# A two-layer retention and sliding-window kernel: splits, loads and statistics in another order

## The reference, cut

```python
def post_norm(res, out, g, b):
    z = DN_ALPHA * res + out
    mu = z.mean(-1, keepdims=True)
    var = jnp.square(z - mu).mean(-1, keepdims=True)
    return (z - mu) * lax.rsqrt(var + LN_EPS) * g + b

def retention_layer(x, w_in, w_out, pos):
    h = x @ w_in                                   # 1024 x 6144
    q, k, v, g = jnp.split(h, [1024, 2048, 4096], axis=-1)
    q = rope(q, pos); k = rope(k, pos) * RET_QK_DIM ** -0.5
    att = einsum('bhncd,bhnmd->bhncm', qc, kc) * dec      # per chunk
    inner = einsum('bhncm,bhnme->bhnce', att, vc)
    def step(state, (qn, kn, vn)):
        cross = einsum('bhcd,bhde->bhce', qn, state) * xi
        state = state * g_chunk + einsum('bhcd,bhce->bhde', kn * zeta, vn)
        return state, cross
    r = inner + cross; r = (r - mean(r)) * rsqrt(var(r) + GN_EPS)   # per head
    return (silu(g) * r) @ w_out                   # 2048 x 1024

def swa_layer(x, w_in, w_out, sinks, k_band, v_band, bias, key_valid):
    q, gate = jnp.split(x @ w_in, 2, axis=-1)      # 1024 x 2048
    sc = where(key_valid, q * SWA_HEAD_DIM ** -0.5 @ k_band + bias, NEG_INF)
    m = maximum(sc.max(-1), sink); p = exp(sc - m)
    o = (p / (p.sum(-1) + exp(sink - m))) @ v_band
    return (o * silu(gate)) @ w_out                # 1024 x 1024
```

## Time and profile before

| | us |
|---|---|
| median of three runs | 2483.75 |
| lowest, highest | 2483.28, 2490.3 |
| profiled execution, device time | 2483.47 |
| profiled execution, span | 2481.5 |

### The profile page before, as it was taken

The page is one execution under the profiler, slowest core; times in us unless marked ns, Lnnn a source line. Parts: engine busy times, 40 slices in busy tenths (PEclk is TensorE's granted clock), DMA queues, the critical chain, the costliest instruction groups (busy, mean ns, idle before and its releaser), DMA issues.

```text
span 2481.5 us, 30993 instructions
## 1 busy us (share of the span) xinstructions
PE 2341.3 (94%) x11506; PEld 1900.2 (77%) x11506; DVE 1812.3 (73%) x2578; ACT 1180.6 (48%) x1754; POOL 345.5 (14%) x352
## 2 busy tenths in 40 slices
PE   7889989989999999999999999999999999999995
PEld 5677777867778887787778888778777888878774
DVE  6977888755886668874697767886478667787457
ACT  3433345346544445534744544443664445553473
POOL 4212201113001110001201001100110110010122
PEclk9999999999999999999999999999999999999998
DMA  9786677571764445744274544575146444464413
GB/s 331 280 294 246 226 240 254 170 280 52 241 199 148 135 129 173 263 148 136 91 268 134 170 158 131 168 256 185 62 153 237 131 141 154 128 203 134 131 60 110
DMA packets 215061, 443.38 MB, mean 179 GB/s; under 512 B 15040, under 2 KB 52432, under 8 KB 211328
## 3 DMA queue, kind: packets, MB, share of 16 engines
q1 hardware_dynamic: 200832, 375.58, 46.1%
q0 software_dynamic: 14080, 65.83, 7.2%
HBM read 379.75 MB, written 57.41 MB: 176 GB/s over the span
## 4 chain that ended last, share of the span: by engine, by line
PE 58%; DVE 15%; issue 12%; DMA 7%; ACT 4%; POOL 2%; SPq 1%; POOLq 0%; DVEq 0%; ACTq 0%
PE accs L644 16%; PE accs L645 15%; PE accs L646 15%; DVE w_lo L1250 5%; DMA stage<-t_prep 4%; PE bank L644 2%; PE bank L646 2%; PE bank L645 2%; ACT w_hi L948 2%; PE bank L866 1%; DMA x_sums<-part_lo 1%; PE bank L875 1%; PE bank L885 1%; PE bank L730 1%; POOL rstd L1830 1%
## 5 line engine op out<-in xcount | busy, mean ns | idle before, releaser
L1250 DVE TENSOR_TENSOR w_lo<-stage,w_hi 128x1024 fp32r<-128x1024 f32 x536 | 670.4, 1255 | 414.3 <-ACT w_hi L948 413.2
L948 ACT ACTIVATE w_hi<-stage 128x1024 fp32r<-128x1024 f32 x536 | 563.6, 1057 | 585.3 <-DMA stage<-t_prep 273.3
L644 PE MATMUL accs<-w_hi,xs 128*128 128x512 f32 x1120 | 450.5, 402 | 45.2 <-DVE krT L1328 12.0
L646 PE MATMUL accs<-w_hi,xs 128*128 128x512 f32 x1120 | 442.6, 395 | 0.0
L645 PE MATMUL accs<-w_lo,xs 128*128 128x512 f32 x1120 | 442.4, 395 | 0.0
L644 PEld LDWEIGHTS accs<-w_hi,xs 128*128 128x128 f32 x1120 | 214.1, 191 | 100.1 <-issue 51.5
L644 PE MATMUL accs<-x_hi,w_hi 128*128 128x512 f32 (+1 forms) x640 | 248.8, 389 | 17.4 <-DVE qT L1714 16.3
L1830 POOL TENSOR_TENSOR rstd<-ve,half 128x1 f32<-128x1 f32 x96 | 80.7, 841 | 1265.1 <-DVE ve L1306 1215.5
L646 PEld LDWEIGHTS accs<-w_hi,xs 128*128 128x128 f32 x1120 | 213.7, 191 | 46.3
L645 PEld LDWEIGHTS accs<-w_lo,xs 128*128 128x128 f32 x1120 | 214.1, 191 | 42.5
L645 PE MATMUL accs<-x_lo,w_hi 128*128 128x512 f32 (+1 forms) x640 | 239.9, 375 | 0.0
(11 more groups left out here) (184 smaller groups left out, 3863.9 us busy)
## 6 DMA issues: line engine op xcount, KB each, us to landing
stage<-t_prep SPq DMA_DIRECT2D x224, 512.0 KB, 4.4
stage<-ret_w_in SPq DMA_DIRECT2D x96, 512.0 KB, 3.9
stage<-ret_w_in SPq DMA_DIRECT2D x128, 256.0 KB, 2.9
stage<-swa_w_in SPq DMA_DIRECT2D x64, 512.0 KB, 3.8
t_prep<-t_buf POOLq DMA_DIRECT2D x28, 1024.0 KB, 6.3
stage<-ret_w_out SPq DMA_DIRECT2D x48, 512.0 KB, 3.7
cs<-rope_t SPq DMA_DIRECT2D x16, 1024.0 KB, 7.6
t_buf<-ret_w_in POOLq DMA_DIRECT2D x32, 512.0 KB, 9.6
```

The lines of the kernel that those rows point to most:

```text
L644: mm(dst, lhs[0], rhs[0], start=start, stop=False, skip_group_check=reopened)
L646: return mm(dst, lhs[1], rhs[0], start=False, stop=stop, skip_group_check=reopened)
L948: copy(w_hi[:, g % HS], stage[:, g % LS], ACT.Copy).then_inc(w_hi_made, 1)
L1250: nc.vector.tensor_tensor(w_lo[:, g % LS], stage[:, g % LS], w_hi[:, g % HS].bitcast(F32), sub).then_inc(w_split, 1)
```

## The change

1. `RO_SPLITS`: split 3 of `ret_w_out`'s operand moves from RO + 5 to RO + 4; ACT's `norm_r(H - 1, 3)` moves from RO + 3 to RO + 4, behind two `copy_r`.
2. Next sums 2 and 3 move from Q0 + 2 and Q0 + 3 to Q1 and Q1 + 1, behind the softmax steps there; their stores move with them.
3. The eight loads of sums at a strip's first pair become two each at pairs 0, 2, 5 and 8.
4. The four part loads wait for the products of RO + 14, 17, 20 and 23.
5. The second layer's norm: the statistics of tile t + 1 stand between gain and bias of tile t (`ln_step`).
6. At RO + 24 the pair's `make_lo` stands between the bias of tile 0 and the gain of tile 1.
7. At SO: split 4 one pair later, the second `o_summed` sum at SO + 2 instead of SO + 1, at SO + 2 the output sum ahead of `make_lo`, at SO + 3 the sum ahead of the split; the half statistics of P2 move from SO + 5 to SO + 9.
8. In the seventh v/gate pair the scores stand ahead of `make_lo`.

The diff, cut (comments and declarations left out; `next_sum_lo` on DVE moves as `next_sum_hi` does on ACT):

```diff
-RO_SPLITS = {61: 0, 63: 1, 65: 2, 77: 3, 78: 4, 80: 5, ...
+RO_SPLITS = {61: 0, 63: 1, 65: 2, 76: 3, 78: 4, 80: 5, ...
-SO_SPLITS = {SO - 2: (0,), SO - 1: (1, 2), SO + 1: (3,), SO + 2: (4,), SO + 4: (5,), SO + 5: (6,), SO + 7: (7,)}
+SO_SPLITS = {SO - 2: (0,), SO - 1: (1, 2), SO + 1: (3,), SO + 3: (4,), SO + 4: (5,), SO + 5: (6,), SO + 7: (7,)}
+NEXT_SUMS = (Q0, Q0 + 1, Q1, Q1 + 1)
+SUM_LOADS = {0: 0, 2: 1, 5: 2, 8: 3}
...
-                    if s > 0 and p == 0:
-                        sp.wait_ge(products, used(s * NP - 1))
-                        wait_sums_stored(sp, s)
-                        for n in range(4):
-                            for hl in range(2):
-                                sp.dma_start(xs[:, X_SUM_SLOT[n], hl].bitcast(F32), x_sums_dram[n, hl])\
-                                    .then_inc(sums_loaded[n], 16)
-                    if s + 1 < NS and Q0 + 1 <= p <= Q0 + 4:
-                        n = p - Q0 - 1
+                    if s > 0 and p in SUM_LOADS:
+                        n = SUM_LOADS[p]
+                        if p == 0:
+                            sp.wait_ge(products, used(s * NP - 1))
+                            wait_sums_stored(sp, s)
+                        for hl in range(2):
+                            sp.dma_start(xs[:, X_SUM_SLOT[n], hl].bitcast(F32), x_sums_dram[n, hl])\
+                                .then_inc(sums_loaded[n], 16)
+                    if s + 1 < NS and p - 1 in NEXT_SUMS:
+                        n = NEXT_SUMS.index(p - 1)
...
-                    if p == RO + 3:
-                        norm_r(H - 1, 3)
                     if p == RO + 4:
                         copy_r(H - 1, 0)
                         copy_r(H - 1, 1)
+                        norm_r(H - 1, 3)
...
-                    if s + 1 < NS and Q0 <= p < Q0 + 4:
-                        next_sum_hi(s, p - Q0)
+                    if s + 1 < NS and p in NEXT_SUMS[:2]:
+                        next_sum_hi(s, NEXT_SUMS.index(p))
...
+                    if s + 1 < NS and p in NEXT_SUMS[2:]:
+                        next_sum_hi(s, NEXT_SUMS.index(p))
...
-                if i == 2 * n + 1:
+                if i == (2 * n + 1 if kind == "ro" else 4 * n + 1):
                     for t in range(2):
                         half_stats(s, kind, "P2", t, 0)
...
+            def ln_step(s, t):
+                dve.wait_ge(gb_loaded, 32 * (2 * s + 2))
+                if t == 0:
+                    ln_begin(s, 1, 0)
                 ln_gain(t)
+                if t + 1 < NT:
+                    ln_begin(s, 1, t + 1)
+                ln_bias(s, 1, t)
+            def ln_two_tiles(s, w, t, g=None):
                 ln_begin(s, w, t)
                 ln_gain(t)
                 ln_begin(s, w, t + 1)
                 ln_bias(s, w, t)
+                if g is not None:
+                    make_lo(g)
                 ln_gain(t + 1)
                 ln_bias(s, w, t + 1)
...
+                    score_first = h < RH and j == VG + 6
+                    if score_first:
+                        evacuate_score(H, 0)
+                        make_lo(g + AHEAD)
...
-                        if v == 6:
-                            evacuate_score(H, 0)
...
-                        ln_two_tiles(s, 0, 0)
-                        make_lo(g + AHEAD)
+                        ln_two_tiles(s, 0, 0, g + AHEAD)
...
                     if SO <= p < SO + 9:
                         output_sums(s, "so", p)
-                    for n in SO_SPLITS.get(p, ()):
-                        split_so(s, n)
-                    if p in (SO, SO + 1, SO + 3):
+                    if p == SO + 2:
+                        make_lo(g + AHEAD)
+                    if p != SO + 3:
+                        for n in SO_SPLITS.get(p, ()):
+                            split_so(s, n)
+                    if p in (SO, SO + 2, SO + 3):
...
+                    if p == SO + 3:
+                        split_so(s, SO_SPLITS[p][0])
...
                 wait_sums_stored(pool, s - 1)
+                pool.wait_ge(products, used((s - 1) * NP + RO + 14 + 3 * n))
```

More of the change, by code:

```diff
@@ L178 @@
             ("P7", 0), ("P7", 1), ("P3", 0), ("P3", 1), ("P4", 0), ("P4", 1)]
-RO_SPLITS = {61: 0, 63: 1, 65: 2, 77: 3, 78: 4, 80: 5, 81: 6, 82: 7, 85: 8, 86: 9, 87: 10, 89: 11, 90: 12, 92: 13}
+RO_SPLITS = {61: 0, 63: 1, 65: 2, 76: 3, 78: 4, 80: 5, 81: 6, 82: 7, 85: 8, 86: 9, 87: 10, 89: 11, 90: 12, 92: 13}
 RO_SUMS = {67: "S3A", 70: "S3B", 71: "S2A", 73: "S4A", 74: "S1A", 79: "S2B", 81: "S1B", 83: "S4B"}
 S3A, S3B, S2A, S4A, S1A, S2B, S1B, S4B = range(1, 9)
-SO_SPLITS = {SO - 2: (0,), SO - 1: (1, 2), SO + 1: (3,), SO + 2: (4,), SO + 4: (5,), SO + 5: (6,), SO + 7: (7,)}
+SO_SPLITS = {SO - 2: (0,), SO - 1: (1, 2), SO + 1: (3,), SO + 3: (4,), SO + 4: (5,), SO + 5: (6,), SO + 7: (7,)}
 TURN_BANK = (4, 6, 7, 4)
+NEXT_SUMS = (Q0, Q0 + 1, Q1, Q1 + 1)
+SUM_LOADS = {0: 0, 2: 1, 5: 2, 8: 3}
 def need(eng, sem, n):
@@ L1528, in ln_bias @@
                                                in1=gb[:, 1, :], op0=ALU.mult, op1=add).then_inc(ln_dve, 1)
-            def ln_tile(s, w, t):
-                dve.wait_ge(gb_loaded, 32 * (2 * s + w + 1))
-                ln_begin(s, w, t)
+            def ln_step(s, t):
+                dve.wait_ge(gb_loaded, 32 * (2 * s + 2))
+                if t == 0:
+                    ln_begin(s, 1, 0)
                 ln_gain(t)
-                ln_bias(s, w, t)
-            def ln_two_tiles(s, w, t):
+                if t + 1 < NT:
+                    ln_begin(s, 1, t + 1)
+                ln_bias(s, 1, t)
+            def ln_two_tiles(s, w, t, g=None):
                 dve.wait_ge(gb_loaded, 32 * (2 * s + w + 1))
@@ L1613, in _ @@
                         rope_k_products(H)
-                    if first_step(p) is None and p not in (RO + 24, KV - 1, KV + 2, KV + 3):
+                    score_first = h < RH and j == VG + 6
+                    if score_first:
+                        evacuate_score(H, 0)
+                        make_lo(g + AHEAD)
+                    if first_step(p) is None and p not in (RO + 24, KV - 1, KV + 2, KV + 3, SO + 2) and not score_first:
                         make_lo(g + AHEAD)
@@ L1619, in _ @@
                     if p < NT and s > 0:
-                        ln_tile(s - 1, 1, p)
+                        ln_step(s - 1, p)
                     if h < RH and j < VG:
@@ L1707, in _ @@
                         make_lo(g + AHEAD + 1)
-                    if s + 1 < NS and Q0 <= p < Q0 + 4:
-                        next_sum_lo(s, p - Q0)
+                    if s + 1 < NS and p in NEXT_SUMS[:2]:
+                        next_sum_lo(s, NEXT_SUMS.index(p))
                     if p in (Q0 + 3, Q1 + 3):
@@ L1747, in _ @@
                             out_, x, y, op = s2v, o_part(1, 4, 8), s3v, sub
-                        elif p == SO + 1:
+                        elif p == SO + 2:
                             dve.wait_ge(o_summed, 4 * s + 2)
```

## The result

| | median us | lowest, highest | runs |
|---|---|---|---|
| before | 2483.5 | 2477.4, 2490.4 | 6 |
| changed | 2464.2 | 2462.7, 2467.0 | 6 |

The ratio of changed to before is 0.9924, with a 95% interval of 0.9909 to 0.9938: 19 us faster, where 47 us were forecast. It lies 1.2 us outside the stated range (2419 to 2463). The profiled execution of the changed kernel took 2462.66 us, with a span of 2460.7 us (before 2481.5), so that the two traces differ by 20.8 us.

What follows compares the result with a forecast made beforehand. TensorE (PE), busy 94% of the span, was taken as the bound, so only its idle time and lower clock could be won. Seven terms summed to 47.2 us off 2483.47, giving 2436 us, range 2419 to 2463.

Steps and rivals of the forecast that it cites:

- Next sums behind the softmax: At Q1, PE's waits for qT shorten as sums 2 and 3 no longer delay ACT and DVE: 12.6 us, clock included.
- Heads of strips: First head, strips 1 to 3: PE's krT waits go, 7.0 us, plus 2.2 of clock in strip 3; together 9.2 us.
- the third rival: Slower: spread x sum loads and part loads meet weights where none met before, 3.78 us each; 2491 us, chance 0.05.
- Scores ahead of a weight split: At the score steps, nine att_lo waits shrink because DVE's weight split no longer stands ahead: 8.1 us.
- Split 3 a pair earlier: Seventh pair of ret_w_out: PE's wait for ra goes in three strips, 0.3 us left in strip 3; 8.5 us.
- Part loads: Stretch of four pairs: loads issued one per three pairs no longer delay weights; 5.5 us, clock included.
- Layer norm at RO + 24: At the 25th pair the w_lo wait goes, but the k/v pair still waits behind bias loads: 1.5 us of 6.7.
- SO: Second layer's output (swa_w_out): z wait of 1.18 us mostly reappears two pairs later; strip 3 wins half statistics; 1.8 us.
- The first rival: Every place is a DVE chain, so what PE gains at one step it waits for next; 2457 us, chance 0.27.

Runs made afterwards that it cites:

- the run of three repairs: Changed kernel with all x sum loads at a strip's first pair, next sums 2 and 3 behind qT at Q0 + 3, state store at RO + 11: 2450.5 us.

## Why the prediction was wrong, point by point

The sum took each wait as won for good, but for those at the k/v pair and at SO, and put what comes back behind the others at nothing. That step failed: by stretches 47.2 us were forecast and 20.8 measured, and of the 26 us that are missing 9.6 lie in the heads, 8.4 in Q0 to G1, 4.6 in RO + 24 to KV and 3.1 in RO + 0 to RO + 15.

- **Next sums behind the softmax** (12.6 us forecast, 4.2 measured over the stretch; the edit itself lost 0.9, and 5.1 came with the sums left in their old place, most of it in strip 2). The first half of the step held: the waits at Q1 fell from 16.3 to 7.5 us (8.0 forecast), and PE's busy time in Q1 of strips 1 and 2 by 4.3 us (4.6 forecast), with the clock back at 1.00. But 6.8 us came back at G0, more than half of it in strip 0. The step that failed is the sentence that ACT and DVE have slack behind softmax steps 0 and 1. No row was read for it, only shares of busy time. The waits of the kernel before had it; of the idle time of both engines in the softmax much is spent on the other one (us in total, times, longest):

```profile
DVE rinv L1593 <- ACT pr L1210: 70.0, 48, 4.8
ACT pr L1210 <- DVE lowest L1586: 52.3, 28, 6.0
```

- **Heads of strips** (9.2 us). krT's waits of strips 1 to 3 went, all 7.0 us. The step that failed is that the first two loads were worked out (3.1 us instead of 12.6) and the other six left to the third rival, as all or nothing at 3.8 us each and 0.05. They cost 1.4 to 3.3 us a strip, 7.6 together: the third rival's mechanism at a fifth of its price, which belonged in the forecast's own term. The reason given for the gain failed, too: weights 9 us earlier were not what the most of krT's waits hung on. With all eight loads back ACT waited 9.06 us again in strip 3 and krT was not waited for; in the run of three repairs it was 11.14 us and 2.2.
- **Scores ahead of a weight split** (8.1 us). Mechanism right, size if anything too small: undoing it costs 9.3 us in two heads. The wait in the first head of strips 1 and 2 stayed at 1.4 us all the same, behind weights that the spread loads made late; with the loads together it is gone. First and fourth head together show 4.5 us of gain only, krT's share in it, since the spread loads took 7.6.
- **Split 3 a pair earlier** (8.5 us; 5.4 measured). The wait went, and 6.2 us came back at RO + 10 in three strips, behind the state's store. The step read the row of the wait, not what transfers are issued in the next pairs. Before, the two weight loads around the store were issued 5.4 us apart, with PE's pause at RO + 6 between them (1003.75 and 1009.10 in strip 1), and now 3.2 us.
- **Part loads** (5.5 us; 5.6 measured). The stretch did come down to strip 3's 21.8 us in every strip. That the number fits is in part luck: with the loads issued at once again only 2.2 us came back, so 3.4 are the other edits', and in strip 0 the spread loads cost 2.3 us at KV.
- **Layer norm at RO + 24** (1.5 us; -3.1). That the wait is passed on to the k/v pairs was right. Its cause I named as the bias loads; in strips 1 and 2 it is DVE's two weight splits ahead of x_lo. The 1.5 us were to come in strip 1, where the k/v pair was to have no wait; it has 1.6 us, and that strip won 0.7. The edit itself is worth zero.
- **SO** (1.8 us; 1.0). Right to the row: the 1.18 us at SO + 4 are gone and 1.41 stand at SO + 6 in every strip, as forecast, and the half statistics won in strip 3 alone.
- **The first rival** was what happened: waits are passed on. It was priced by choosing which terms survive whole, at 2457 us; the mechanism took from nearly all of them. At 0.27 it was too unlikely, and with its own spread should have set the upper end of the range.

## What to carry to other kernels

In a kernel whose matrix engine is 94% busy, a wait removed is worth the distance to the next thing that is late, and this has to be read at the pairs behind it: which transfers are issued in them, and whether an idle engine waits for another that the moved work lengthens. In this kernel bulk loads were cheapest where a step lasts long and the lead covers them all at once, not spread over the short steps: spreading cost 7.6 us for the x sums and won 2.2 in its stretch for the part loads, for which ACT had been waiting (5.45 us). That the used-up lead makes the difference between the two is a reading, not shown by a run. When half of a gain is missing, undo the edits one by one and compare the stretch, not the whole time.

## What the runs showed that I had not expected

- Transfers of 512 KB landed 4.8 and 4.9 us after their issue (median, strip 2) with eight loads in a burst some pairs ahead of them, and 7.6 us with two loads spread in among them, although the first head moves 237 GB/s with the burst and 227 with the spread.
- The same pause, 1.9 us at RO + 6, went with a clock of 1.00 in three strips before and of 0.97 in two of these three with split 3 put back, and busy time was 1.3 and 1.6 us longer in those two. The earlier trace rows has 0.88 with one wait of 1.87 us in the window. So one execution can be off by that much a strip through the clock alone.
- Moving two small groups of loads (bias, and the second layer's gain and bias) by a few pairs was worth 13 us, 2450.5 to 2437.6; the whole change was worth 19.
